# The last value unit of each feed-forward stage, worked through in thirds of the tokens

## The chip, the cores and the metric

The kernel runs on one core of a Trainium2 chip. The metric is the device time of one execution in microseconds (us); lower is better. The time of the kernel before is a median of three runs. Beside them there is one execution that the hardware profiler recorded. The engines are TensorE (PE, matrix products), VectorE (DVE), ScalarE (ACT), GpSimd (POOL) and SyncE (SP, which issues the transfers).

## The reference

One inference step of a decoder of two layers, for 1024 prompt tokens and 8 sample tokens, 1032 columns in all, in float32. Each layer is an attention mixer with a residual, and then a convolutional feed-forward with a residual. The change touches only the feed-forward:

```python
def conv_ffn(hn, conv_state, w_up, conv_w, conv_b, w_down):
    T = hn.shape[1]
    u = hn @ w_up                                             # D 1024 -> 2 * 2816
    uc = jnp.concatenate([conv_state.astype(u.dtype), u], axis=1)
    c = sum((conv_w[j] * uc[:, j:j + T] for j in range(CONV_W)), conv_b)   # causal, width 3
    gate, val = jnp.split(c, 2, axis=-1)
    return (jax.nn.silu(gate) * val) @ w_down, uc[:, T:]
```

## The kernel before

Features lie on the 128 partitions and tokens on the free axis. The residual `hT` is 8 chunks of 128 features by 1032 tokens. A float32 product is made of three matmuls on operands that are split into a high and a low part (`product`, lines 348 to 350: high by high, high by low, low by high), each over one third of the tokens (`TH` = 344 columns, `NT` = 3). The PSUM tensor `acc` has two sets of three banks, `acc_set(0)` and `acc_set(1)`, one bank for each third.

The 2816 inner features are 22 chunks. A feed-forward stage takes them two at a time, in 11 turns; `ffn_pe`, `ffn_act` and `ffn_dve` run the same turn on their engines, ten times as a loop and once, the last (`z.last`), written out. There are two stages, one for each layer. A turn holds four up units (the gate and the value half of two chunks; one unit is 72 matmuls) and two down units. In the last turn three up units are left, numbered 1 (value), 2 (gate) and 3 (value).

What one unit goes through after its matmuls, in the kernel before, always over the full 1032 tokens:

- ACT copies it out of PSUM into `u_ext` (L1090).
- DVE scales it by the norm's `rinv` (L1140), and makes the convolution: one tensor_scalar with the last tap and the bias (L1142), one tensor by scalar plus tensor for each of the two other taps (L1145, L1149), two small ones on the 8 sample tokens (L1147, L1152), and a small copy of the last columns into `u_tail` (L1143).
- For a gate unit ACT then makes the SiLU (L1095) into `ebuf`. For a value unit DVE multiplies it with `ebuf` into `fbuf` (L1159), ACT rounds that into `f_hi` (L1098), and DVE takes the rest into `f_lo` (L1161).

The down products read `f_hi` and `f_lo`. For each of 8 output chunks n and each third t there are three matmuls for the turn's first inner chunk (e = 0) and three for its second (e = 1), into `acc_set(n % 2)`. DVE adds the finished set to `hT` (L882). Chunk n + 2 needs the set that chunk n used, so its matmuls wait for that addition (`h_added`). In the last turn the matmuls of e = 0 for the chunks n = 0 and 1 are issued ahead (`early = 2`), since they need only the first inner chunk; then TensorE waits for `flo_ready` of the second (line 1056) before any matmul of e = 1.

Each engine works strictly in the order of its program; the order is written out by hand, and semaphores carry what waits for what.

Of the kernel before, what the change touches and what calls it, by code (L numbers as in the profile page):

```python
# [29 lines left out]
KC = D // P  # L30
SEQ = 1024
NS = 8
T = SEQ + NS
NT = 3
TH = T // NT
# [77 lines left out]
def build(nc, a, outs):  # L113
    with ExitStack() as ctx:
# [3 lines left out]
        def sem(name):  # L118
            return ctx.enter_context(nc.semaphore(name))
# [52 lines left out]
        tab_in = sem("tab_in")  # L172
        conv_in = sem("conv_in")
        gain_rows_set = sem("gain_rows_set")
        gains_turned = sem("gains_turned")
        gains_set = sem("gains_set")
        tab_turned = sem("tab_turned")
        tab_set = sem("tab_set")
# [29 lines left out]
        up_evac = sem("up_evac")  # L208
        conv_step = sem("conv_step")
        u_scaled = sem("u_scaled")  # L210
        conv_out = sem("conv_out")
        e_ready = sem("e_ready")
        f_raw = sem("f_raw")
# [9 lines left out]
        chain = sem("chain")  # L223

        class Dilated:

# [54 lines left out]
        class Sample:  # L281

            def __init__(self, p, slots):
                self.cols = sem(f"{p}_cols")
                self.cache = [sem(f"{p}_cache{i}") for i in range(slots)]
                self.prep = sem(f"{p}_prep")
                self.moved = sem(f"{p}_moved")
                self.kt = sem(f"{p}_kt")
                self.step = sem(f"{p}_step")
                self.act = sem(f"{p}_act")  # L290
                self.pe = sem(f"{p}_pe")
                self.out = sem(f"{p}_out")
# [4 lines left out]
                self.split = sem(f"{p}_split")  # L297
# [98 lines left out]
        def acc_set(n):  # L396
            return acc[:, 3 * (n % 2):3 * (n % 2) + 3, 0:TH]
# [72 lines left out]
        def rows_in_pe(pe):  # L470
            pe.wait_ge(ident_in, 16)
            for n in range(NTILE + 1):
                pe.wait_ge(x_in[n % XS], 16 * (n // XS + 1))
                if n >= 3:
                    pe.wait_ge(h_set, 2 * (n - 3) + 2)
                rows = P if n < NTILE else NS
                for c in range(KC):
                    mm = pe.transpose(acc[:, (2 * n + c // 4) % 6, P * (c % 4):P * (c % 4) + rows],
                                      x_stage[n % XS][0:rows, P * c:P * c + P], ident[0:rows, 0:rows])
                mm.then_inc(x_turned, 1)  # L480
            pe.wait_ge(tab_in, GAINS_IN)
            pe.transpose(aux[:, 1, 0:46], head_rows, ident[0:46, 0:46])
            pe.transpose(aux[:, 1, 64:64 + 5 * KC], norm_rows, ident[0:5 * KC, 0:5 * KC]) \
                .then_inc(gains_turned, 1)

        def conv_tables_pe(pe, n):

# [20 lines left out]
        def rows_in_dve(v):  # L508

            v.memset(head_rows, 1.0).then_inc(gain_rows_set, 1)  # L510
            for n in range(NTILE + 1):
                v.wait_ge(x_turned, n + 1)
                rows = P if n < NTILE else NS
                for b in range(2):
                    v.tensor_copy(hT[:, 4 * b:4 * b + 4, P * n:P * n + rows],
                                  acc[:, (2 * n + b) % 6, :].rearrange("p (c n) -> p c n", n=P)[:, :, 0:rows]) \
                        .then_inc(h_set, 1)
            v.wait_ge(gains_turned, 1)
# [107 lines left out]
        def third(x, t):  # L626
            return x[:, TH * t:TH * t + TH]
# [386 lines left out]
                body(eng, Turn(l, i, False))  # L1014
            body(eng, Turn(l, LAST, True))

        def up_pe(pe, unit, k):
            slot, u, _ = unit_at(*unit)
            pe.wait_ge(lo_ready, u + 1)
            w1 = w_hi[:, slot, :].rearrange("p (k n) -> p k n", n=P)  # L1020
            w2 = w_lo[:, slot, :].rearrange("p (k n) -> p k n", n=P)
            for t in range(NT):
                for j in range(KC):
                    mm = product(pe, acc_set(k)[:, t, :], w1[:, j, :], w2[:, j, :], third(xh[:, j, :], t),
                                 third(xl[:, j, :], t), j == 0, j == KC - 1)
            mm.then_inc(w_used, 1)

        def ffn_turn_pe(pe, z):
            pe.wait_ge(h_added, z.added - 1)
# [12 lines left out]

            def down(n, e, t):
                s = slots[e]
                return product(pe, acc_set(k0 + n)[:, t, :], w_hi[:, s, P * n:P * n + P],
                               w_lo[:, s, P * n:P * n + P], third(f_hi[:, e, :], t), third(f_lo[:, e, :], t),
                               e == 0, e == 1)


            early = 2 if z.last else 0  # L1050
            pe.wait_ge(flo_ready, z.f + 1)
            for n in range(early):
                pe.wait_ge(up_evac, z.up + n + 3)
                for t in range(NT):
                    down(n, 0, t)
            pe.wait_ge(flo_ready, z.f + 2)
            for n in range(KC):
                if n >= 2:
                    pe.wait_ge(h_added, z.added + n - 1)
                elif not z.last:  # L1060
                    pe.wait_ge(up_evac, z.up + n + 4)
                for t in range(NT):
                    if n >= early:
                        m0 = down(n, 0, t)
                    m1 = down(n, 1, t)
                if n < KC - 1:
                    m1.then_inc(res_full, 1)
                else:
                    m0.then_inc(w_used, 1)
                    m1.then_inc(w_used, 1)  # L1070

        def ffn_pe(pe, l):
            u0 = [U_FFN0, U_FFN1][l]
            pe.wait_ge(lo_ready, u0 + 1)
            *_, mm = normed_product(pe, u0 % RING, 1 + 3 * l)
            mm.then_inc(w_used, 1)
            pe.wait_ge(n_stat, 2 * STAT[1 + 3 * l] + 1)
            turns(pe, l, ffn_turn_pe)

            pe.wait_ge(conv_out, UPS * (l + 1))  # L1080
            pe.wait_ge(tail_set, 2 * l)
# [10 lines left out]
        def gate_act(act, z, e):  # L1092
# [4 lines left out]
            act.wait_ge(w_used, z.no(1))  # L1097
            act.copy(f_hi[:, e, :], fbuf).then_inc(fhi_ready, 1)  # L1098

        def ffn_turn_act(act, z):  # L1100
            split_ahead(act, *z.unit(1))
            up_evac_act(act, z, 1, VAL, 1)
# [4 lines left out]
            up_evac_act(act, z, 3, VAL, 1)  # L1107
            if not z.last:
                split_ahead(act, *z.unit(4))
            gate_act(act, z, 1)  # L1110
            if not z.last:
# [42 lines left out]
        def gated_dve(v, z, e):  # L1154
# [5 lines left out]
            v.wait_ge(fhi_ready, z.f + e + 1)  # L1160
            v.tensor_tensor(f_lo[:, e, :], fbuf, f_hi[:, e, :].bitcast(F32), ALU.subtract).then_inc(flo_ready, 1)  # L1161

        def ffn_turn_dve(v, z):
# [5 lines left out]
            conv_dve(v, l, z.up + 3, VAL, FC + g + 1, s + CONV_STEPS, z.f + 1)  # L1169
            gated_dve(v, z, 1)  # L1170
            s += 2 * CONV_STEPS
            k0 = 0 if z.last else 1
            for n in range(KC):
# [11 lines left out]

        def ffn_dve(v, l):
            for n in range(2):
                v.memset(u_ext[n][:, 0:2], 0.0).then_inc(chain, 1)
            v.wait_ge(chain, 2 * (l + 1))
# [1468 lines left out]
```

## Time and profile before

| | us |
|---|---|
| median of three runs | 2930.18 (2929.76 to 2930.49) |
| profiled execution | 2925.12 |
| its span | 2923.3 |
| TensorE busy in the span | 2695.3 (92%) |
| VectorE busy | 1802.5 (62%) |
| ScalarE busy | 979.7 (34%) |
| GpSimd busy | 729.4 (25%) |

Busy time says how long an engine had an instruction under way. The span is from the first to the last instruction of the profiled execution; 1.8 us of its time lie around it. TensorE's granted clock over the span is 0.951 of its full 2.4 GHz. On this chip it has two levels, 1.2 and 2.4 GHz; at a third of the tokens (344 columns) the matmuls start 0.157 us apart at the upper one and 0.287 us apart at the lower one. The first feed-forward stage's last turn lies around 1640 to 1686 us, the second's around 2855 to 2900 us, just before the rows of the result are turned and written.

### The profile page before, as it was taken

To read this page: it belongs to the slowest core of one execution; us is meant where nothing else is said; L and a number is where in the kernel's file an instruction comes from. 1 tells how busy PE (TensorE), PEld (TensorE's weight loads), DVE (VectorE), ACT (ScalarE), POOL (GpSimd) and SP (SyncE) were. 2 spreads that over 40 slices of the span, in tenths; PEclk is the share of its full clock that TensorE was granted. 3 is DMA by queue.
4 is the path that set the end of the run, shared out by engine and by line. 5 is a ranking of instruction groups with operands and counts; after the bars stand their busy time and mean duration, and the time that the engine had idled before them with its cause. 6 is when DMAs were issued, how large, how long until landed. Compare 5 with 4: busy or idle time off the path is not lost.

```text
span 2923.3 us, 45840 instructions
## 1 busy us (share of the span) xinstructions
PE 2695.3 (92%) x17524; PEld 2626.7 (90%) x17524; DVE 1802.5 (62%) x2804; ACT 979.7 (34%) x1818; POOL 729.4 (25%) x354
## 2 busy tenths in 40 slices
PE   4999999788788999999999969698999999999997
PEld 3999999777778999999999958598999999999996
DVE  6787831555545666666666686795266666666665
ACT  3666632666304211212211245584131111211220
POOL 2111112344302222222222141173222222222220
PEclk7999999888788999999999989898999999999998
DMA  3322233434345333444444111444634444444341
GB/s 105 86 79 85 74 123 95 151 107 113 107 145 113 84 89 84 83 96 95 88 90 92 38 40 59 130 145 127 133 80 89 90 89 85 83 85 93 86 76 61
DMA packets 219857, 275.65 MB, mean 94 GB/s; under 512 B 29562, under 2 KB 191746, under 8 KB 217666
## 3 DMA queue, kind: packets, MB, share of 16 engines
q1 hardware_dynamic: 219746, 274.17, 38.1%
q8 instruction: 70, 1.15, 0.2%
q14 instruction: 41, 0.34, 0.0%
HBM read 237.90 MB, written 125.62 MB: 124 GB/s over the span
## 4 chain that ended last, share of the span: by engine, by line
PE 75%; DVE 9%; issue 5%; ACT 4%; DMA 3%; POOL 2%; SPq 1%; DVEq 0%; ACTq 0%; POOLq 0%
PE acc L348 21%; PE acc L350 21%; PE acc L349 21%; PE aux L2019 2%; DVE arena L609 1%; PE aux L1614 1%; PE acc L2006 1%; DVE f_lo L1161 1%; DVE arena L1140 1%; DVE arena L1159 1%; PE acc L1539 1%; PE acc L1989 1%; PE aux L666 1%; PE aux L665 1%; PE acc L1573 1%
## 5 line engine op out<-in xcount | busy, mean ns | idle before, releaser
L348 PE MATMUL acc<-xh,w_hi 128*128 128x344 f32 x3504 | 1136.8, 324 | 47.4 <-DVE xl L563 21.7
L350 PE MATMUL acc<-xh,w_lo 128*128 128x344 f32 x3504 | 1128.8, 322 | 0.0
L349 PE MATMUL acc<-xl,w_hi 128*128 128x344 f32 x3504 | 1128.5, 322 | 0.0
L333 POOL TENSOR_TENSOR w_lo<-w_raw,w_hi 128x1024 fp32r<-128x1024 f32 x194 | 499.9, 2582 | 1810.4 <-ACT w_hi L323 1810.4
L348 PEld LDWEIGHTS acc<-xh,w_hi 128*128 128x128 f32 x3504 | 666.0, 190 | 61.5 <-issue 31.2
L350 PEld LDWEIGHTS acc<-xh,w_lo 128*128 128x128 f32 x3504 | 666.3, 190 | 0.0
L349 PEld LDWEIGHTS acc<-xl,w_hi 128*128 128x128 f32 x3504 | 665.9, 190 | 0.2
L882 DVE TENSOR_TENSOR hT<-hT,acc 128x1032 f32<-128x1032 f32 x184 | 226.3, 1230 | 388.2 <-PE acc L350 388.2
L323 ACT CAST w_hi<-w_raw 128x1024 fp32r<-128x1024 f32 x194 | 201.8, 1051 | 603.1 <-PE acc L350 515.2
L348 PE MATMUL acc<-f_hi,w_hi 128*128 128x344 f32 x1056 | 342.2, 324 | 29.2 <-DVE f_lo L1161 29.2
L350 PE MATMUL acc<-f_hi,w_lo 128*128 128x344 f32 x1056 | 340.5, 322 | 0.0
L349 PE MATMUL acc<-f_lo,w_hi 128*128 128x344 f32 x1056 | 339.4, 321 | 0.0
L1140 DVE TENSOR_TENSOR arena<-arena,rinv 128x1032 f32<-128x1032 f32 x88 | 146.5, 1665 | 175.9 <-ACT arena L1090 159.7
L1090 ACT COPY arena<-acc 128x1032 f32<-128x1032 f32 x86 | 87.9, 1022 | 446.6 <-PE acc L350 446.6
L1142 DVE TENSOR_SCALAR arena<-arena,cw 128x1032 f32<-128x1032 f32 x88 | 227.5, 2586 | 15.9 <-DVE arena L1140 15.6
L348 PEld LDWEIGHTS acc<-f_hi,w_hi 128*128 128x128 f32 x1056 | 200.3, 190 | 35.4 <-issue 21.2
L350 PEld LDWEIGHTS acc<-f_hi,w_lo 128*128 128x128 f32 x1056 | 200.2, 190 | 0.0
L349 PEld LDWEIGHTS acc<-f_lo,w_hi 128*128 128x128 f32 x1056 | 200.1, 189 | 0.0
L1098 ACT CAST f_hi<-arena 128x1032 fp32r<-128x1032 f32 x44 | 46.5, 1056 | 289.7 <-DVE arena L1159 289.7
L1145 DVE SCALAR_TENSOR_TENSOR arena<-arena,cw 128x1024 f32<-128x1024 f32 x88 | 113.1, 1285 | 4.8
L1149 DVE SCALAR_TENSOR_TENSOR arena<-arena,cw 128x1024 f32<-128x1024 f32 x88 | 113.0, 1284 | 0.2
L1838 ACT ACTIVATE arena<-arena 128x128 f32<-128x128 f32 (+1 forms) x192 | 84.6, 445 | 13.4 <-DVE arena L1679 13.3
(264 smaller groups left out, 3147.3 us busy)
## 6 DMA issues: line engine op xcount, KB each, us to landing
out_a_w_sample<-in_cache_a_kv_w SPq DMA_DIRECT2D x23, 2848.0 KB
w_raw<-in_ffn_w_up SPq DMA_DIRECT2D x88, 512.0 KB, 3.9
scratch<-arena SPq DMA_DIRECT2D x46, 516.0 KB, 3.1
w_raw<-in_ffn_w_down SPq DMA_DIRECT2D x44, 512.0 KB, 3.5
w_raw<-in_a_w_in SPq DMA_DIRECT2D x36, 512.0 KB, 4.3
out_a_w_sample<-in_cache_a_kv_w SPq DMA_DIRECT2D x8, 2044.0 KB
arena<-in_cache_a_kv_w SPq DMA_DIRECT2D x24, 512.0 KB, 3.8
w_raw<-scratch SPq DMA_DIRECT2D x17, 512.0 KB, 3.8
```

What stands on the lines that cost most here:

```text
L323: act.copy(w_hi[:, slot, :], w_raw[:, slot, :]).then_inc(hi_ready, 1)
L333: pool.tensor_tensor(w_lo[:, slot, :], w_raw[:, slot, :], w_hi[:, slot, :].bitcast(F32), ALU.subtract).then_inc(lo_ready, 1)
L348: pe.matmul(out, whi, ahi, start=first, stop=False)
L349: pe.matmul(out, whi, alo, start=False, stop=False)
L350: return pe.matmul(out, wlo, ahi, start=False, stop=last)
L882: v.tensor_tensor(thirds(hT[:, n, :]), thirds(hT[:, n, :]), acc_set(k), ALU.add).then_inc(h_added, 1)
L1090: act.copy(thirds(u_ext[which][:, 2:U1]), acc_set(k)).then_inc(up_evac, 1)
L1140: v.tensor_tensor(u[:, 2:U1], u[:, 2:U1], rinv[:], ALU.mult).then_inc(u_scaled, 1)
L1142: v.tensor_scalar(c[:, 0:T], u[:, 2:U1], w[2], w[3], ALU.mult, ALU.add).then_inc(conv_step, 1)
L1145: v.scalar_tensor_tensor(c[:, 0:SEQ], u[:, 1:SEQ + 1], w[1], c[:, 0:SEQ], ALU.mult, ALU.add) \
L1149: v.scalar_tensor_tensor(c[:, 0:SEQ], u[:, 0:SEQ], w[0], c[:, 0:SEQ], ALU.mult, ALU.add) \
L1838: act.activation(y, y, ACT.Exp, bias=stat_col(i, g, 0, h, t), scale=-1.0, accum_out=stat_col(i, g, 1, h, t)).then_inc(DA.exped, 1)
```

## The change

In the last turn of each stage, the chain behind up unit 3 is done by thirds of the tokens. TensorE signals after each third of the unit (`last_full`). ACT copies third 0 and third 1 out as they are finished, while the unit's later matmuls still run. DVE scales, convolves and multiplies a third, ACT rounds it, DVE subtracts, and TensorE's e = 1 matmuls for n = 0 and 1 are issued by thirds, each with its own wait. The other ten turns, and the chunks n = 2 to 7 of the last one, are as before. The copy into `u_tail` moves to the end of the chain, and the transposes behind the stage wait for it too. Three semaphores that were in use elsewhere are merged or dropped to make room (`gains_turned`, `chain`, an unused one); the steps of the chain count on `ffn_once`.

On VectorE, at the last turn of the second stage, the rows from the scaling of unit 3 to its residual addition read in the kernel before:

```order
L1140 TENSOR_TENSOR arena<-arena,rinv 128x1032 [waits f_raw,up_evac]
L1142 TENSOR_SCALAR arena<-arena,cw 128x1032 [waits u_scaled]
L1143 COPY u_tail<-arena 128x10
L1145 SCALAR_TENSOR_TENSOR arena<-arena,cw 128x1024 [waits conv_step]
L1147 SCALAR_TENSOR_TENSOR arena<-st_T,cw,arena 128x8
L1149 SCALAR_TENSOR_TENSOR arena<-arena,cw 128x1024 [waits conv_step]
L1152 SCALAR_TENSOR_TENSOR arena<-st_T,cw,arena 128x8 [waits conv_step]
L1159 TENSOR_TENSOR arena<-arena 128x1032 [waits flo_ready,e_ready,conv_out]
L1161 TENSOR_TENSOR f_lo<-arena,f_hi 128x1032 [waits fhi_ready]
```

In the changed kernel the five rows of third 0 and the four of third 1's convolution stand ahead (L1226, L1228, L1230, L1233 are the convolution of a third, L1258 its product with the gate), and from the `f_lo` of third 0 (L1266) on it reads:

```order
L1266 TENSOR_TENSOR f_lo<-arena,f_hi 128x344 [waits last_act]
L1258 TENSOR_TENSOR arena<-arena 128x344 [waits flo_ready,e_ready,ffn_once]
L1238 TENSOR_TENSOR arena<-arena,rinv 128x344 [waits up_evac]
L1240 TENSOR_SCALAR arena<-arena,cw 128x344 [waits u_scaled]
L1242 SCALAR_TENSOR_TENSOR arena<-arena,cw 128x336 [waits conv_step]
L1244 SCALAR_TENSOR_TENSOR arena<-st_T,cw,arena 128x8
L1246 SCALAR_TENSOR_TENSOR arena<-arena,cw 128x336 [waits conv_step]
L1248 SCALAR_TENSOR_TENSOR arena<-st_T,cw,arena 128x8 [waits conv_step]
L1266 TENSOR_TENSOR f_lo<-arena,f_hi 128x344 [waits last_act]
L1258 TENSOR_TENSOR arena<-arena 128x344 [waits e_ready,flo_ready,conv_step,conv_out]
L1266 TENSOR_TENSOR f_lo<-arena,f_hi 128x344 [waits fhi_ready]
L1281 COPY u_tail<-arena 128x10
```

Nine rows of the full width have become twenty-one, and the `f_lo` of a third stands one step late, behind the convolution of the next third, so that ACT can round it meanwhile.

On ScalarE, at the same place, the kernel before has the copy out of unit 3, the SiLU of unit 2 and the rounding of unit 3:

```order
L1090 COPY arena<-acc 128x1032 [waits conv_out,w_used]
L1095 ACTIVATE arena<-arena 128x1032 [waits f_raw,conv_out]
L1098 CAST f_hi<-arena 128x1032 [waits w_used,f_raw]
```

and the changed one:

```order
L1130 COPY arena<-acc 128x344 [waits conv_out,last_full] x2
L1146 ACTIVATE arena<-arena 128x1032 [waits f_raw,conv_out]
L1138 CAST f_hi<-arena 128x344 [waits ffn_once,w_used]
L1130 COPY arena<-acc 128x344 [waits conv_out,w_used]
L1138 CAST f_hi<-arena 128x344 [waits ffn_once]
L1138 CAST f_hi<-arena 128x344 [waits f_raw]
```

The SiLU now stands ahead of the copy of the last third, and the rounding of third 0 between them. The core of the diff:

```diff
@@ up_pe: a signal after each third
+                if by_third and t < NT - 1:
+                    mm.then_inc(last_full, 1)
@@ ffn_turn_pe
-            up_pe(pe, z.unit(3), 1)
+            up_pe(pe, z.unit(3), 1, z.last)
...
-            pe.wait_ge(flo_ready, z.f + 2)
-            for n in range(KC):
+            if z.last:
+                for t in range(NT):
+                    if t < NT - 1:
+                        pe.wait_ge(ffn_once, steps(z.l, f"lo{t}"))
+                    else:
+                        pe.wait_ge(flo_ready, z.f + 2)
+                    for n in range(early):
+                        m1 = down(n, 1, t)
+                        if t == NT - 1:
+                            m1.then_inc(res_full, 1)
+            else:
+                pe.wait_ge(flo_ready, z.f + 2)
+            for n in range(early, KC):
                 if n >= 2:
                     pe.wait_ge(h_added, z.added + n - 1)
@@ new on ScalarE
+        def last_half_act(act, z):
+            last_evac_act(act, z, 0)
+            last_evac_act(act, z, 1)
+            act.wait_ge(conv_out, z.up + 3)
+            act.wait_ge(f_raw, z.f + 1)
+            act.activation(ebuf, cg, ACT.Silu).then_inc(e_ready, 1)
+            act.wait_ge(w_used, z.no(1))
+            last_hi_act(act, z, 0)
+            last_evac_act(act, z, 2)
+            last_hi_act(act, z, 1)
+            last_hi_act(act, z, 2)
@@ new on VectorE: the convolution of thirds 0 and 1
+                v.wait_ge(last_act, acts(l, f"evac{t}"))
+                n = steps(l, f"conv{t}")
+                v.tensor_tensor(last_third(u, t), last_third(u, t), third(rinv, t), ALU.mult).then_inc(ffn_once, 1)
+                v.wait_ge(ffn_once, n + 1)
+                v.tensor_scalar(third(c, t), last_third(u, t), w[2], w[3], ALU.mult, ALU.add).then_inc(ffn_once, 1)
+                v.wait_ge(ffn_once, n + 2)
+                v.scalar_tensor_tensor(c[:, a:b], u[:, 1 + a:1 + b], w[1], c[:, a:b], ALU.mult, ALU.add) \
+                    .then_inc(ffn_once, 1)
...
+        def last_half_dve(v, z, ch, s):
+            v.wait_ge(f_raw, z.f + 1)
+            last_conv_dve(v, z, ch, s, 0)
+            last_product_dve(v, z, 0)
+            last_conv_dve(v, z, ch, s, 1)
+            last_lo_dve(v, z, 0)
+            last_product_dve(v, z, 1)
+            last_conv_dve(v, z, ch, s, 2)
+            last_lo_dve(v, z, 1)
+            last_product_dve(v, z, 2)
+            last_lo_dve(v, z, 2)
+            v.tensor_copy(u_tail[:, :, bass.ds(ch, 1)], u_ext[VAL][:, SEQ:U1].unsqueeze(2)).then_inc(ffn_once, 1)
@@ ffn_turn_act and ffn_turn_dve call them where z.last, and the old steps otherwise
```

## Rows read from the trace of the kernel before

**Rows 1.** Waits of TensorE: who waited for whom, us, times, longest.
```profile
PE acc L348 <- DVE f_lo L1161: 29.2, 22, 6.8
```

**Rows 2.** Timeline of TensorE, second stage: start us, us, engine line op [idle before].
```profile
2855.57 0.32 PE L348 MATMUL acc<-xh,w_hi 128*128 128x344 f32 x1
...
2866.75 0.32 PE L350 MATMUL acc<-xh,w_lo 128*128 128x344 f32 x1
...
2869.57 0.32 PE L350 MATMUL acc<-f_hi,w_lo 128*128 128x344 f32 x1
2876.71 0.66 PE L348 MATMUL acc<-f_hi,w_hi 128*128 128x344 f32 x1 [6.82 <-DVE f_lo L1161]
2877.16 0.49 PE L349 MATMUL acc<-f_lo,w_hi 128*128 128x344 f32 x1
```

**Rows 3.** Timeline of VectorE, second stage, same columns.
```profile
2863.45 0.23 DVE L1152 SCALAR_TENSOR_TENSOR arena<-st_T,cw,arena 128x8 f32<-128x8 f32 x1
2868.16 1.23 DVE L1140 TENSOR_TENSOR arena<-arena,rinv 128x1032 f32<-128x1032 f32 x1 [4.49 <-ACT arena L1090]
2869.43 0.82 DVE L1142 TENSOR_SCALAR arena<-arena,cw 128x1032 f32<-128x1032 f32 x1
...
2870.28 1.28 DVE L1145 SCALAR_TENSOR_TENSOR arena<-arena,cw 128x1024 f32<-128x1024 f32 x1
2871.48 0.22 DVE L1147 SCALAR_TENSOR_TENSOR arena<-st_T,cw,arena 128x8 f32<-128x8 f32 x1
...
2873.07 1.23 DVE L1159 TENSOR_TENSOR arena<-arena 128x1032 f32<-128x1032 f32 x1
2875.42 1.23 DVE L1161 TENSOR_TENSOR f_lo<-arena,f_hi 128x1032 fp32r<-128x1032 f32 x1 [1.12 <-ACT f_hi L1098]
2879.70 1.23 DVE L882 TENSOR_TENSOR hT<-hT,acc 128x1032 f32<-128x1032 f32 x1 [3.04 <-PE acc L350]
...
2885.11 1.23 DVE L882 TENSOR_TENSOR hT<-hT,acc 128x1032 f32<-128x1032 f32 x1 [1.61 <-PE acc L350]
```

**Rows 4.** Timeline of ScalarE, second stage, same columns.
```profile
2867.11 1.02 ACT L1090 COPY arena<-acc 128x1032 f32<-128x1032 f32 x1 [9.36 <-PE acc L350]
2868.02 1.07 ACT L1095 ACTIVATE arena<-arena 128x1032 f32<-128x1032 f32 x1
2874.34 1.05 ACT L1098 CAST f_hi<-arena 128x1032 fp32r<-128x1032 f32 x1 [5.24 <-DVE arena L1159]
```

**Rows 5.** Lines with a third's width: duration ns min/median/max, first and last start.
```profile
L698 DVE TENSOR_TENSOR f_lo<-arena,f_hi x99: 516/518/520, 75.6 to 1871.5; 128x344 fp32r<-128x344 f32 x99
L717 DVE TENSOR_TENSOR arena<-aux,rope x99: 503/517/518, 78.9 to 1875.0; 128x344 f32<-128x344 f32 x99
L696 DVE CAST f_hi<-arena x99: 326/332/791, 74.8 to 1871.1; 128x344 fp32r<-128x344 f32 x99
L720 DVE TENSOR_TENSOR arena<-arena x99: 516/518/2564, 79.5 to 1875.6; 128x344 f32<-128x344 f32 x99
L677 ACT ACTIVATE arena<-acc x99: 441/457/460, 73.8 to 1868.0; 128x344 f32<-128x344 f32 x99
L680 ACT CAST f_hi<-arena x99: 478/480/484, 74.8 to 1869.0; 128x344 fp32r<-128x344 f32 x99
```

**Rows 6.** Timeline of GpSimd in the last turns, same columns as rows 2.
```profile
1661.66 2.47 POOL L333 TENSOR_TENSOR w_lo<-w_raw,w_hi 128x1024 fp32r<-128x1024 f32 x1 [16.09 <-ACT w_hi L323]
2857.82 2.50 POOL L333 TENSOR_TENSOR w_lo<-w_raw,w_hi 128x1024 fp32r<-128x1024 f32 x1 [8.83 <-ACT w_hi L323]
```

**Rows 7.** Timeline of VectorE, first stage: the addition of chunk 2.
```profile
1670.26 1.23 DVE L882 TENSOR_TENSOR hT<-hT,acc 128x1032 f32<-128x1032 f32 x1 [1.68 <-PE acc L350]
```

**Rows 8.** Stretches: us, busy (x instructions) by engine, granted clock, DMA share, GB/s.
```profile
908.90:912.70 3.80, 1.82 (x11) 1.40 (x9) 2.91 (x4) 3.80 (x5) 0.00 (x0) 1.00 0.77 96
912.70:914.57 1.87, 0.00 (x0) 0.00 (x0) 1.87 (x3) 1.87 (x3) 0.00 (x0) 1.00 1.54 195
916.10:919.60 3.50, 3.50 (x14) 3.50 (x14) 3.50 (x4) 2.13 (x3) 0.00 (x0) 0.52 1.20 169
1655.10:1660.10 5.00, 0.03 (x1) 0.00 (x0) 4.42 (x7) 0.51 (x1) 0.00 (x0) 1.00 0.00 0
2869.90:2871.90 2.00, 0.00 (x0) 0.00 (x0) 2.00 (x5) 0.00 (x0) 0.00 (x0) 0.99 0.00 0
2871.90:2876.70 4.80, 0.00 (x0) 0.00 (x0) 3.60 (x4) 1.05 (x1) 0.00 (x0) 0.50 0.00 0
2876.70:2882.04 5.34, 5.33 (x19) 5.33 (x20) 1.23 (x1) 0.00 (x0) 0.00 (x0) 0.50 0.00 0
```

More of the change, by code:

```diff
@@ L210, in build, with acts, steps @@
         u_scaled = sem("u_scaled")
+        last_full, last_act, ffn_once = sem("last_full"), sem("last_act"), sem("ffn_once")
+        ACTS = {"evac0": 1, "evac1": 2, "hi0": 3, "hi1": 4}
+        STEPS = {"set": 2, "conv0": 2, "raw0": 7, "conv1": 7, "lo0": 12, "raw1": 13, "lo1": 14, "tail": 15}
+        def acts(l, name):
+            return len(ACTS) * l + ACTS[name]
+        def steps(l, name):
+            return STEPS["tail"] * l + STEPS[name]
         conv_out = sem("conv_out")
@@ L222, in build @@
         copied = sem("copied")
-        chain = sem("chain")
         class Dilated:
@@ L1015, in turns, with up_pe @@
             body(eng, Turn(l, LAST, True))
-        def up_pe(pe, unit, k):
+        def up_pe(pe, unit, k, by_third=False):
             slot, u, _ = unit_at(*unit)
@@ L1080, in ffn_pe @@
             pe.wait_ge(conv_out, UPS * (l + 1))
+            pe.wait_ge(ffn_once, steps(l, "tail"))
             pe.wait_ge(tail_set, 2 * l)
@@ L1098, in gate_act, with last_third, last_evac_act, last_hi_act @@
             act.copy(f_hi[:, e, :], fbuf).then_inc(fhi_ready, 1)
+        def last_third(x, t):
+            return x[:, 2 + TH * t:2 + TH * t + TH]
+        def last_evac_act(act, z, t):
+            if t < NT - 1:
+                act.wait_ge(last_full, (NT - 1) * z.l + t + 1)
+            else:
+                act.wait_ge(w_used, z.no(3) + 1)
+            act.wait_ge(conv_out, z.up + 2)
+            act.copy(last_third(u_ext[VAL], t), acc_set(1)[:, t, :]) \
+                .then_inc(last_act if t < NT - 1 else up_evac, 1)
+        def last_hi_act(act, z, t):
+            if t < NT - 1:
+                act.wait_ge(ffn_once, steps(z.l, f"raw{t}"))
+            else:
+                act.wait_ge(f_raw, z.f + 2)
+            act.copy(third(f_hi[:, 1, :], t), third(fbuf, t)).then_inc(last_act if t < NT - 1 else fhi_ready, 1)
+        def last_half_act(act, z):
[9 more added lines that the diff above has]
+            last_hi_act(act, z, 2)
         def ffn_turn_act(act, z):
@@ L1106, in ffn_turn_act @@
             split_ahead(act, *z.unit(3))
-            up_evac_act(act, z, 3, VAL, 1)
-            if not z.last:
+            if z.last:
+                last_half_act(act, z)
+            else:
+                up_evac_act(act, z, 3, VAL, 1)
                 split_ahead(act, *z.unit(4))
-            gate_act(act, z, 1)
-            if not z.last:
+                gate_act(act, z, 1)
                 up_evac_act(act, z, 4, GATE, 0)
@@ L1161, in gated_dve, with last_conv_dve @@
             v.tensor_tensor(f_lo[:, e, :], fbuf, f_hi[:, e, :].bitcast(F32), ALU.subtract).then_inc(flo_ready, 1)
+        def last_conv_dve(v, z, ch, s, t):
+            l, u, c = z.l, u_ext[VAL], c_out[VAL]
+            w = [cw[:, l, k, bass.ds(ch, 1)] for k in range(4)]
+            state = [st_T[:, l, :, bass.ds(ch + 2 * FC * k, 1)] for k in range(2)]
+            a, b = TH * t, min(TH * t + TH, SEQ)
+            if t < NT - 1:
+                v.wait_ge(last_act, acts(l, f"evac{t}"))
[6 more added lines that the diff above has]
+                    .then_inc(ffn_once, 1)
+                v.wait_ge(ffn_once, n + 3)
+                v.scalar_tensor_tensor(c[:, a:b], u[:, a:b], w[0], c[:, a:b], ALU.mult, ALU.add) \
+                    .then_inc(ffn_once, 1)
+                return
+            cs = c[:, SEQ:T].unsqueeze(2)
+            v.wait_ge(up_evac, z.up + 4)
+            v.tensor_tensor(last_third(u, t), last_third(u, t), third(rinv, t), ALU.mult).then_inc(u_scaled, 1)
+            v.wait_ge(u_scaled, z.up + 4)
+            v.tensor_scalar(third(c, t), last_third(u, t), w[2], w[3], ALU.mult, ALU.add).then_inc(conv_step, 1)
+            v.wait_ge(conv_step, s + 1)
+            v.scalar_tensor_tensor(c[:, a:b], u[:, 1 + a:1 + b], w[1], c[:, a:b], ALU.mult, ALU.add) \
+                .then_inc(conv_step, 1)
+            v.scalar_tensor_tensor(cs, state[1], w[1], cs, ALU.mult, ALU.add).then_inc(conv_step, 1)
+            v.wait_ge(conv_step, s + 2)
+            v.scalar_tensor_tensor(c[:, a:b], u[:, a:b], w[0], c[:, a:b], ALU.mult, ALU.add).then_inc(conv_step, 1)
+            v.wait_ge(conv_step, s + 3)
+            v.scalar_tensor_tensor(cs, state[0], w[0], cs, ALU.mult, ALU.add).then_inc(conv_out, 1)
@@ new lines, in last_product_dve @@
+        def last_product_dve(v, z, t):
+            if t < NT - 1:
+                v.wait_ge(ffn_once, steps(z.l, f"conv{t}") + 4)
+            else:
+                v.wait_ge(conv_out, z.up + 4)
+                v.wait_ge(conv_step, TURN_STEPS * FFN_TURNS * (z.l + 1))
+            v.wait_ge(e_ready, z.f + 2)
+            v.wait_ge(flo_ready, z.f + 1)
+            v.tensor_tensor(third(fbuf, t), third(cv, t), third(ebuf, t), ALU.mult) \
+                .then_inc(ffn_once if t < NT - 1 else f_raw, 1)
@@ L1168, in ffn_turn_dve @@
             conv_dve(v, l, z.up + 2, GATE, g + 1, s, z.f + 1)
-            conv_dve(v, l, z.up + 3, VAL, FC + g + 1, s + CONV_STEPS, z.f + 1)
-            gated_dve(v, z, 1)
+            if z.last:
+                last_half_dve(v, z, FC + g + 1, s + CONV_STEPS)
+            else:
+                conv_dve(v, l, z.up + 3, VAL, FC + g + 1, s + CONV_STEPS, z.f + 1)
+                gated_dve(v, z, 1)
             s += 2 * CONV_STEPS
@@ L1187, in ffn_dve @@
             for n in range(2):
-                v.memset(u_ext[n][:, 0:2], 0.0).then_inc(chain, 1)
-            v.wait_ge(chain, 2 * (l + 1))
+                v.memset(u_ext[n][:, 0:2], 0.0).then_inc(ffn_once, 1)
+            v.wait_ge(ffn_once, steps(l, "set"))
             v.wait_ge(n_stat, 2 * STAT[1 + 3 * l] + 2)
```

13 lines of the change are left out of this document (9 added, 4 removed).

## The prediction, on record before the changed kernel ran

> **What bounds the kernel now.** I read the list of waits of TensorE first, since that engine is busy for 92% of the span and most of the chain that ended last is its matmuls. In it the wait of the first down matmul (L348) for the last step of the feed-forward chain (L1161) is the largest: 29.2 us, 22 times, at most 6.8 us [rows 1]. The 22 are the 11 turns of both stages. The two last turns hold 6.8 us each, 13.6 in all, so the other twenty have 0.8 us each. The change touches only those two.
>
> Then I read the timelines of the second stage's last turn, engine by engine. TensorE starts up unit 3 at 2855.57 and issues the last of its 72 matmuls at 2866.75, 0.157 us apart; 18 matmuls of e = 0 follow, until 2869.57; then nothing until 2876.71 [rows 2]. In that gap everything runs one after another over the full width: copy out on ACT from 2867.11, scaling from 2868.16, three wide steps of the convolution and two small ones, the product from 2873.07, the rounding on ACT from 2874.34, the subtraction from 2875.42 to 2876.65 [rows 3, 4]. Before it VectorE had been idle for 4.49 us, from 2863.68, the end of the gate's convolution [rows 3]: the finished thirds of unit 3 lay in PSUM and nobody took them. That idle time is what the change can use.
>
> The gap costs more than its length. The granted clock falls to 0.50 inside it, and stays there for the first 5.34 us of matmuls, in which 18 are issued 0.287 us apart instead of 0.157 [rows 2, 8]. So 18 x 0.13 = 2.3 us belong to the gap too.
>
> **The change, part by part.** All times are of the second stage.
>
> Durations of a third. A tensor by tensor step takes 0.518 us, a copy from PSUM on ACT 0.457, a rounding on ACT 0.480 [rows 5]. The tensor by scalar plus tensor step takes 1.28 us at 1024 columns and 0.22 at 8 [rows 3]; on the straight line between, 344 columns take 0.57. The trace has no tensor_scalar with two scalars at 344 columns. It is at least 0.33 us, as the cheapest single-input step of that width [rows 5], and at most 0.82, as at 1032 columns with GpSimd idle [rows 3]; I take 0.46: the wide one is 0.41 us below the wide tensor by tensor step, so I give it half of that step's 1.04 ns a column (1.233 less 0.518 over 688 columns), and 688 columns fewer take 0.36 off 0.82. A step that waits for the one before it starts 0.04 us after its end; one that doesn't wait starts 0.08 before it (2869.39 to 2869.43, and 2870.28 + 1.28 against 2871.48) [rows 3].
>
> ACT copies third 0 out near 2859.5 and third 1 at 2863.3 (the unit's thirds are 24 matmuls, 3.77 us, apart, and the last ends at 2867.07) [rows 2]; both are out when VectorE comes free. Then the SiLU, 2863.8 to 2864.9: it used to stand behind the copy and now stands ahead of it, and is ready before third 0 needs it.
>
> VectorE, third 0: scaling from 2863.60, tensor_scalar 2864.16, two taps 2864.66 and 2865.28, product 2865.89 to 2866.41. ACT rounds it until 2866.93 and then copies third 2 out, 2867.11 to 2867.57, as early as before. The rounding stands ahead of that copy: were the product of third 0 later than about 2866.6, the copy would be late; there is 0.2 us of room, then 0.7 until chunk 1's e = 0 matmuls want the bank near 2868.3, and 1.8 until VectorE wants third 2. Third 1: scaling 2866.33, its convolution until 2868.58, the subtraction of third 0 from 2868.50 to 2869.02, the product 2868.94 to 2869.46. Third 2: scaling 2869.38, tensor_scalar 2869.94, the taps with the two small steps until 2871.77, the subtraction of third 1 until 2872.21, the product 2872.13 to 2872.65, rounding until 2873.17, subtraction 2873.21 to 2873.73.
>
> TensorE: third 0 (6 matmuls, 0.94 us) is ready at 2869.02, before e = 0 is through; it goes from 2869.73 to 2870.67. Third 1 from 2872.25 to 2873.2. Third 2 from 2873.78, against 2876.71 before for all 18: the chain is 2.9 us shorter although VectorE does more instructions (21 for 9) and 2.4 us more of work.
>
> The new wait. Chunk 2 needs the set of chunk 0, so it needs its addition. Before, 9 matmuls of chunk 1 covered that: addition 0 began at 2879.70 and chunk 2 at 2882.08 (2885.11 less 0.04, 0.32 and 17 x 0.157) without waiting [rows 3]. Now only 3 matmuls lie between. After a wait the second matmul follows 0.45 us behind instead of 0.287 [rows 2], so I add 0.16. Chunk 0 is full at 2873.78 + 0.16 + 2 x 0.157 + 0.32 = 2874.57, its addition runs 2874.62 to 2875.85 (the tail's copy, 0.17, is over by then), and chunk 2 starts at 2875.90, after about a microsecond of waiting. Queued behind that wait are all other down matmuls, so it counts in full. The addition of chunk 2 then begins at 2875.90 + 0.16 + 17 x 0.157 + 0.36 = 2879.09. It was 2885.11: 6.0 us less, if the clock stays up. From there on both kernels are paced by 18 matmuls a chunk, 2.83 us.
>
> First stage: the same turn 1214.76 us earlier, and its addition of chunk 2 is at 1670.26 [rows 7] against 2879.09 - 1214.76 = 1664.33 now: 5.9 us less. What is different there is the weight split of the next stage's first unit on GpSimd. It runs 2.47 us from 1661.66 [rows 6], behind the last rounding and one cast on ACT, and would run from about 1659.5, over the addition of chunk 0. Steps of VectorE with two SBUF operands are held up by such a thing, up to 2564 ns instead of 518, but the same step with one operand in PSUM never was, 503 to 518 ns over 99 [rows 5]; the addition reads PSUM, so I take 0. In the second stage GpSimd is idle from 2860.32 on [rows 6], ahead of all thirds. The squares of the next norm, the loads and the transposes follow the additions as before and move with them. The transposes' new wait for the tail's copy is met 25 us ahead. The merged semaphores, 20 more signals and the weight loads cost nothing on the path. The copies by thirds on ACT lie in 9.36 us of idle time [rows 4].
>
> Sum: 6.0 + 5.9 = 11.9 us off the profiled execution, 2925.12 to 2913.2. The median of the runs is 5.06 us above that execution; I carry this over: 2930.18 - 11.9 = 2918.2.
>
> **A rule against the rows: the clock.** The pauses that are left are 1.6 us (after third 0), 0.6 (after third 1) and 1.0 (before chunk 2), with 0.94 us of matmuls between. In the trace the clock fell 2.0 us after the last matmul in the second stage and only after 5.0 us in the first [rows 8]. And from 908.9 to 916.1 matmuls with pauses below 2.0 us between them first kept 1.00, then fell to the lower level at about 916.1, behind a pause of 1.87 us [rows 8]. So pauses of this size can cost the clock, but don't have to. The Trainium skill (TensorE: Matmul & The Clock Gate, HAM oscillation) puts the fall behind single idle gaps that are longer than any left here; by it no stage would fall and the time is the 2918.2 of the sum. The row at 916.1 does not agree with that, and by it one stage in three may fall. I go by the row for the chances, and by no fall in either stage for the likeliest.
>
> **The rivals.** (1) The clock falls in one stage or both, between third 0 and chunk 2. Price: 5.34 us were needed to get it back [rows 8], in which 18 matmuls lose 0.13 each: 2.4 us a stage. 2920.6 for one, 2923.0 for both. For it: the row at 916.1. Against: more matmuls stand in the gap than there.
> (2) The small steps cost more than their widths say (waits that cross engines at each third, the tensor_scalar at 0.82). 21 steps at 0.1 us more make third 2 2.1 us late, 4.2 us over both stages: 2922.4. For it: nothing here shows these shapes with three semaphores on one step. Against: the hand-overs of 0.04 us.
> (3) The gain of the first stage is lost behind it, in the transfers and stores between the layers: only 6.0 us remain, 2924.2. Against: that part starts by semaphores from the last addition, and no transfer is waited for within it before the projections.
> (4) Slower than before. The clock falls in the first pause and does not come back while chunks 2 to 7 run, because each of them now starts on a TensorE that has just waited. Price: 0.13 us for each of their 108 matmuls, 14.0 us a stage, against the 6.0 gained; from 46 matmuls at the low clock on the stage loses. One stage: 2930.18 - 11.9 + 14.0 = 2932.3. Against it: in both stages of before the clock came back within 5.4 us of unbroken matmuls, and from chunk 3 on nothing breaks them.
> (5) That the thirds change nothing, since VectorE was not free: excluded by its 4.49 us of idle time.
>
> **How the numbers follow.** Forecast with no fall in either stage 0.43; (1) 0.36, of which 0.28 for one stage; (2) 0.10; (3) 0.07; (4) 0.04. Below about 0.2% (5.9 us) a measurement of this kernel can't tell a change from none. Faster by more: the forecast, (1) and (2), 0.89. Within: (3) and a mixture of (1) and (2), 0.07. Slower: 0.04. The range: if the tensor_scalar takes its 0.33 and the 0.16 after a wait is hidden, a stage gains 0.6 more, 2917.0, and 1 us for the scatter of the median gives 2916.0. Above it takes in both falls and half of (2): 2923.6.
>
> **What would show it.** In the profile after, the wait of TensorE for L1161's place should fall from 6.8 us a stage to two waits of about 1.6 and 0.6, and a new one of 1.0 for the addition of chunk 0 appears. The step of third 0 should be over before e = 0 is through, third 2 should be ready 2.9 us earlier, and 12 of the 18 matmuls should lie ahead of it. The granted clock should stay at 1.00 from 2855 to the rows' output. The addition of chunk 2 should come 6.0 us earlier. It is wrong if a wide wait stays (VectorE's steps dearer), if the clock drops, or if the two stages gain unequally.

## The result, and the profile after

| | before | changed |
|---|---|---|
| median, us | 2929.97 (8 runs, 2927.93 to 2932.99) | 2918.37 (8 runs, 2913.69 to 2925.10) |
| ratio | | 0.9959, 95% interval 0.9950 to 0.9968 |
| profiled execution | 2925.12 | 2924.54 |

The changed kernel is 11.6 us faster, by the medians; the interval allows 9.4 to 14.6. The change was compared twice more: 2917.91 against 2933.40 (ratio 0.9963, interval 0.9935 to 0.9992) and 2918.73 against 2929.51 (0.9956, 0.9940 to 0.9972), 15.5 and 10.8 us by the medians.

The two profiled executions differ by 0.6 us only, and a reader who compared their spans would find no gain. Single executions of one kernel scatter by several us, in parts of the program that the change doesn't touch. The start of the copy of unit 2 in the first stage's last turn is a mark for that. It lies ahead of everything that is done by thirds; of the change only the merged semaphores lie earlier. It is at 1641.02 us in the first trace of before, 1645.15 in a second one, 1647.78, 1649.09 and 1643.03 in three of the changed kernel; over all 14 traces of this study it lies between 1640.8 and 1652.7. One stretch in which the traces part, in the trace of before, in a second trace of before and in that of the changed kernel (stretch, busy by engine, then granted clock, DMA share, GB/s):

```profile
840.00:930.00 90.00, 81.85 (x500) 80.03 (x501) 30.35 (x37) 26.23 (x27) 12.06 (x6) 0.86 0.52 128
```
```profile
840.00:930.00 90.00, 79.25 (x478) 76.51 (x479) 32.06 (x44) 22.73 (x25) 11.95 (x5) 0.82 0.50 128
```
```profile
840.00:930.00 90.00, 77.67 (x471) 75.03 (x472) 33.53 (x48) 22.23 (x24) 12.63 (x6) 0.81 0.50 130
```

In all 14 traces the mark is later, the fewer matmuls lie in this stretch: from 502 and 1640.8 us down to 454 and 1652.7. From 930 to 1640 us all of them have the same work at a clock of 1.00. So this scatter arises ahead of 930 us, 700 us before the changed turn, and kernels with and without the change are mixed along the row.

So I measure the change where it acts: in each stage's last turn, from the start of the copy of up unit 2 to the start of the addition of chunk 2. I call this the stretch. In the second stage of before it is 2855.77 to 2885.11, 29.34 us, and 29.24 in the first. VectorE in the second stage of the changed kernel (start us, us, engine, line; ahead of these, third 0 began at 2869.37 right behind the gate's convolution):

```profile
2874.21 0.52 DVE L1266 TENSOR_TENSOR f_lo<-arena,f_hi 128x344 fp32r<-128x344 f32 x1
2874.64 0.51 DVE L1258 TENSOR_TENSOR arena<-arena 128x344 f32<-128x344 f32 x1
2875.07 0.51 DVE L1238 TENSOR_TENSOR arena<-arena,rinv 128x344 f32<-128x344 f32 x1
2875.61 0.46 DVE L1240 TENSOR_SCALAR arena<-arena,cw 128x344 f32<-128x344 f32 x1
2876.11 0.57 DVE L1242 SCALAR_TENSOR_TENSOR arena<-arena,cw 128x336 f32<-128x336 f32 x1
...
2878.83 0.52 DVE L1266 TENSOR_TENSOR f_lo<-arena,f_hi 128x344 fp32r<-128x344 f32 x1 [0.55 <-ACT f_hi L1138]
2879.26 0.17 DVE L1281 COPY u_tail<-arena 128x10 f32<-128x10 f32 x1
2880.17 2.37 DVE L888 TENSOR_TENSOR hT<-hT,acc 128x1032 f32<-128x1032 f32 x2 [0.74 <-PE acc L356]
2884.59 1.23 DVE L888 TENSOR_TENSOR hT<-hT,acc 128x1032 f32<-128x1032 f32 x1 [2.05 <-PE acc L356]
```

These answer to [rows 3]. VectorE has no idle time of 4.49 us any more. The last subtraction ends at 2879.35, and the copy of unit 2 began at 2861.55 in this trace, 5.78 us later than in that of before. With this taken off ("on the clock of before", below), the end is 2873.57, against 2876.65: 3.1 us earlier. The stretch is 23.04 us. TensorE around it:

```profile
2876.32 0.32 PE L356 MATMUL acc<-f_hi,w_lo 128*128 128x344 f32 x1
2877.91 0.43 PE L354 MATMUL acc<-f_hi,w_hi 128*128 128x344 f32 x1 [1.28 <-DVE f_lo L1266]
...
2879.40 0.42 PE L354 MATMUL acc<-f_hi,w_hi 128*128 128x344 f32 x1 [0.29 <-DVE f_lo L1266]
2879.66 0.32 PE L355 MATMUL acc<-f_lo,w_hi 128*128 128x344 f32 x1
...
2881.45 0.42 PE L354 MATMUL acc<-f_hi,w_hi 128*128 128x344 f32 x1 [0.85 <-DVE hT L888]
```

One pause of 6.82 us [rows 2] has become three, before third 1, before third 2, and before chunk 2, which waits for the addition of chunk 0. (The times in brackets count from the end of the last matmul, which a profile models, and so come out 0.16 us below a pause counted from when the next matmul could have started.) In the first stage the same three stand (1.27, 0.28 and 0.46), but the clock falls in the middle, 0.4 us after the matmuls of third 2 have begun. Stretches of the first stage, then of the second (us, busy PE, PEld, DVE, ACT, POOL, granted clock, DMA, GB/s):

```profile
1662.70:1666.00 3.30, 1.75 (x10) 1.30 (x9) 2.41 (x8) 1.43 (x2) 0.00 (x0) 1.00 0.00 0
1666.00:1669.40 3.40, 2.94 (x11) 2.50 (x10) 2.37 (x2) 1.50 (x2) 2.38 (x1) 0.51 0.00 0
2876.50:2882.00 5.50, 3.08 (x16) 2.39 (x16) 4.22 (x10) 0.48 (x1) 0.00 (x0) 1.00 0.00 0
```

The first stage's stretch is 24.00 us, from 1647.78 to 1671.78. The two stages gain 5.24 and 6.30, together 11.54 us.

Does this reach the end of the program? From the start of the copy of unit 2 in the second stage to the end of the span it is 67.4 to 67.7 us in three traces whose second stage is as before, and 61.2 to 61.3 in four whose second stage works by thirds: 6.2 us less, all of it. From that copy in the first stage to the one in the second it is 1214.7 to 1217.3 us in three traces with the first stage as before, and 1210.7 to 1213.8 in four with the first stage by thirds. The means are 3.9 us apart, with a scatter of 3 us in each group, so this shows that the first stage's gain gets through, but not how much of it.

### The profile page after: what moved, and what is told of

Read it like the earlier page. It is cut to its first block, busy times and chain, and to the rows that moved or that the text cites. A ratio compares the mean times of both kernels' runs of the same rounds, so it can differ in the third digit from the quotient of the medians.

```text
span 2922.8 us, 45882 instructions
## 1 busy us (share of the span) xinstructions
PE 2701.8 (92%) x17524; PEld 2633.1 (90%) x17524; DVE 1804.8 (62%) x2828; ACT 982.1 (34%) x1826; POOL 729.3 (25%) x354
## 4 chain that ended last, share of the span: by engine, by line
PE 74%; DVE 10%; issue 5%; ACT 3%; DMA 3%; POOL 2%; SPq 1%; DVEq 0%; ACTq 0%; POOLq 0%
PE acc L354 21%; PE acc L356 21%; PE acc L355 20%; PE aux L2142 2%; PE aux L1737 1%; DVE arena L615 1%; PE acc L1662 1%; PE acc L2129 1%; DVE arena L1194 1%; PE acc L1705 1%; PE acc L2112 1%; PE aux L672 1%; DVE f_lo L1215 1%; DVE arena L1213 1%; PE aux L671 1%
```

## The experiments

The stretches below are read from each kernel's own trace, as above. Before, in two traces: 29.24 and 28.94 in the first stage, 29.34 and 29.41 in the second. The second trace was taken in the expectation that the stretch repeats within 0.2 us; in the first stage it moved by 0.3.

**The changed kernel again.** No edit.

> The changed kernel once more, for its scatter and a second trace. My theory (each stage gains about 6: third 2 is ready 2.9 us earlier, 12 of 18 matmuls lie ahead of it, the low clock behind the stall goes, one new wait of about 1 us): 11 to 12 us below the kernel before. If the scatter of the single executions (2914 to 2925) comes from this change, the two stages' last turns will differ by several us from those of the first trace; if it comes from elsewhere, they repeat within 1.2 us (the price of one short stay at the low clock) and the differences lie in the attention parts.

> The changed kernel beside the three variants below, on one chip: stretch 24.0 and 23.1 us again, and a third look at whether the clock falls in the first stage's pauses and not in the second's.

Medians as above. Stretches 23.99 and 23.08, then 23.11 and 23.06. So the change's own part repeats within 0.1 us but for the first stage, where the clock fell in two traces of three and not in the third: 24.0 or 23.1. The third trace was expected to show the fall again and did not. The mark ahead of the change moved by 6 us meanwhile. The scatter of the executions is from elsewhere.

**One stage only.** The condition `z.last` of the new code is made `z.last and z.l == 0`, or `== 1`; the counts of the semaphores follow.

> Thirds in the first stage's last turn only, the second stage as before. My theory: 5.2 to 5.9 us below the kernel before (2924.5). Rival, that what the first stage gains is lost again in the transfers and waits between the layers: 0 to 1 us below.

> Thirds in the second stage's last turn only. My theory: 6.0 us below the kernel before (2924.2). Rival, that the first stage gives nothing and all of the gain is here: 11 us below.

Measured 2925.16 and 2927.63 against 2933.40: ratios 0.9971 (0.9951 to 0.9991) and 0.9976 (0.9958 to 0.9994), 8.2 and 5.8 us. Stretches 23.99 and 29.23 in the one, 29.26 and 23.04 in the other: each stage gains where it is changed and only there. The intervals of the times are wide, but the first stage's gain does reach the end: the rival that it is lost between the layers would have wanted a ratio of 0.9997 or more there. The other rival, 11 us from the second stage alone, lies inside the second interval (1.8 to 12.3 us) and is refuted by the stretches, not by the time.

**TensorE waits for the whole second chunk.**

```diff
+            pe.wait_ge(flo_ready, z.f + 2)
             if z.last:
-                for t in range(NT):
... (the waits and the issue by thirds)
-            for n in range(early, KC):
+                pe.wait_ge(ffn_once, steps(z.l, "lo1"))
+            for n in range(KC):
```

The matmuls of e = 1 are then issued chunk by chunk, as before.

> ACT and VectorE work by thirds as in the change, but TensorE takes the second inner chunk only when all its thirds are there, and then chunk by chunk as before. The pause of TensorE is then one of 3.9 us instead of 6.8, with all 18 matmuls behind it, and no wait for the first addition. My theory: the shorter chain alone gives 2.9 us a stage; if the low clock goes as well, 5.3 us a stage. So 5.8 us below the kernel before if the clock still falls in both, 10.6 if in neither. Rival, that the issue by thirds is the larger part of the gain: no more than 5.8 below even where the trace shows the clock at 1.00.

Measured 2925.90 against 2933.40, ratio 0.9976 (0.9953 to 0.9999), 7.5 us. Stretches 25.41 and 25.35: 3.9 us a stage, between my two values. The trace of the second stage says why:

```profile
2876.50:2880.40 3.90, 0.18 (x3) 0.01 (x1) 3.28 (x10) 0.63 (x2) 0.00 (x0) 1.00 0.00 0
2880.40:2882.00 1.60, 1.60 (x9) 1.60 (x10) 0.03 (x1) 0.00 (x0) 0.00 (x0) 0.94 0.00 0
2882.00:2885.40 3.40, 3.40 (x14) 3.40 (x14) 1.80 (x2) 0.00 (x0) 0.00 (x0) 0.53 0.00 0
```

The clock falls, but not in the pause: 1.4 us after the matmuls have begun again (0.4 in the first stage), so that 12 matmuls run at the lower level and not 18: 1.6 us and not 2.3. Both theories missed that the price depends on where the fall lies. The last subtraction ends at 2873.56 on the clock of before, as in the change. 29.34 less 3.1 for the chain less 0.8 for the six matmuls more at the upper level is 25.4, as measured. So the shorter chain alone is half of the gain. The rival, a small gain even with the clock at 1.00, was not put to the test, since the clock fell in both stages. The stretch of the change with the clock up, 23.06, is 2.3 us below this: 1.6 for the clock, and 0.7 left for the 12 matmuls that lie ahead (1.9) less the new wait and the restarts.

**The clock by itself.** In the kernel before, after the e = 0 matmuls of the last turn:

```diff
+            def filler(count):
+                for _ in range(count):
+                    pe.matmul(aux[:, 0, 0:TH], w_hi[:, slots[0], 0:P], third(f_hi[:, 0, :], 0), start=True, stop=True)
...
+            if z.last:
+                filler(42)
             pe.wait_ge(flo_ready, z.f + 2)
```

> The kernel before, with 42 matmuls of no use (6.6 us, into a free PSUM bank) in the pause of each last turn, nothing else. They shorten no chain. My theory: the clock stays at 1.00 and the 18 matmuls behind are issued 0.157 us apart; the stretch becomes 26.9 us in both stages, 4.6 us in all below before. So 2.3 of the 6 us a stage are the clock's. Rival, that the low clock only accompanies the stall and costs nothing of its own (VectorE sets the pace behind it): 29.2 still.

Measured 2923.80 against 2932.48, ratio 0.9973 (0.9955 to 0.9991), 8.7 us, with 4.6 inside the interval (2.6 to 13.2). Stretches 27.16 and 27.10. The chain is as long as ever, and TensorE meets its end with the clock up:

```profile
2883.82 1.74 PE L1052 MATMUL aux<-f_hi,w_hi 128*128 128x344 f32 x10
2885.77 0.42 PE L348 MATMUL acc<-f_hi,w_hi 128*128 128x344 f32 x1 [0.21 <-DVE f_lo L1167]
2886.03 0.32 PE L349 MATMUL acc<-f_lo,w_hi 128*128 128x344 f32 x1
2886.19 0.32 PE L350 MATMUL acc<-f_hi,w_lo 128*128 128x344 f32 x1
```

So 2.1 to 2.2 us of each stage's stretch of 29.3 were the clock's (1.8 to 2.3 by the second trace of before), and the rival that it costs nothing is refuted. Behind the stage this trace does not keep all of it: from the copy of unit 2 to the end of the span it is 66.7 us against 67.5, because one transfer was issued 1.7 us behind the one before it, where the same one follows after 0.4 us in before. That is one issue in one trace, and no run says what held it up.

**The splitting without the overlap.**

```diff
 def last_evac_act(act, z, t):
     if t < NT - 1:
         act.wait_ge(last_full, (NT - 1) * z.l + t + 1)
-    else:
-        act.wait_ge(w_used, z.no(3) + 1)
+    act.wait_ge(w_used, z.no(3) + 1)
```

> As the changed kernel, but ACT copies all three thirds out only after the whole of unit 3 (the wait of third 2 also ahead of thirds 0 and 1). So the splitting stays and the overlap with unit 3 goes. My theory: the chain of 10.1 us now starts at 2867.56 instead of 2863.60 and ends 1.1 us later than before's; 12 matmuls lie ahead of its end, so the stretch is 27.1 us with the clock up and up to 29.5 with it down. 0 to 4.4 us below before in all. Rival, that splitting into thirds alone gives the gain: a stretch of 25 us or less.

Measured 2926.17 against 2932.48, ratio 0.9979 (0.9962 to 0.9996), 6.3 us. Stretches 27.25 and 27.16. TensorE's waits in the second stage (us, times, longest):

```profile
PE acc L354 <- ACT arena L1129: 3.0, 1, 3.0
PE acc L354 <- DVE f_lo L1265: 1.1, 2, 0.8
PE acc L354 <- DVE hT L888: 0.9, 1, 0.9
```

and the end of its chain on VectorE:

```profile
2868.41 0.52 DVE L1225 TENSOR_TENSOR arena<-arena,rinv 128x344 f32<-128x344 f32 x1 [4.03 <-ACT arena L1129]
...
2877.87 0.52 DVE L1265 TENSOR_TENSOR f_lo<-arena,f_hi 128x344 fp32r<-128x344 f32 x1 [0.55 <-ACT f_hi L1137]
```

The idle time of VectorE is back. The copy of unit 2 is at 2856.48 here, so the chain ends at 2877.68 on the clock of before, 1.0 us later than the whole-width one, as worked out, and 4.1 us later than in the change. Some 2.1 us of the gain stay without overlap; the other 4.1 a stage (27.16 less 23.06) come from taking the thirds while the unit still runs. The rival, a stretch of 25 us or less, is refuted. What I had not seen is the wait of 3.0 us: chunk 1's e = 0 matmuls need the bank set, and the copy of third 2 now stands behind the rounding of third 0, which waits for VectorE. The clock fell as well, in the first stage by the end of this wait, in the second 0.8 us behind it:

```profile
2872.90:2875.90 3.00, 3.00 (x12) 2.79 (x11) 2.93 (x8) 0.48 (x1) 0.00 (x0) 0.52 0.01 3
```

Yet the stretches are those of my sum with the clock up (27.1). Behind the slow matmuls TensorE still waited 0.8 us (0.6 in the first stage) for the subtraction of third 1, so their slowness went into that wait. Here a low clock cost nothing, since nothing waited for these matmuls.

**What the new wait and the fall of the clock cost.** Three variants of the changed kernel. In the first the addition of chunk 0 is done in two parts, third 0 in VectorE's idle 0.55 us ahead of the last subtraction; in the second 8, 2 and 5 matmuls of no use stand in the three pauses; the third has both (8, 2 and 3).

```diff
... (a signal behind chunk 0's third 0 on PE; ACT counts 3 signals a stage, not 2)
             last_product_dve(v, z, 2)
+            v.wait_ge(last_full, NT * z.l + NT)
+            h = third(hT[:, 0, :], 0)
+            v.tensor_tensor(h, h, acc_set(0)[:, 0, :], ALU.add)
             last_lo_dve(v, z, 2)
... (the later addition of chunk 0 takes its thirds 1 and 2 only)
@@ PE, behind the e = 1 matmuls of each third
+                    filler((8, 2, 3)[t])
```

> Only the addition of chunk 0's third 0 is put ahead, no matmuls of no use. My theory: 0.35 us less in each stage: stretch 23.7 and 22.7, with the clock low for some 3.4 us in the first stage as in the change. Rival, that the shorter pause alone keeps the clock up: 22.7 in both.

> Only the matmuls of no use (8, 2 and 5) are put into the pauses of the changed kernel. My theory: the clock stays at 1.00 in both stages and the stretch is 23.1 in both: 0.9 us less in the first stage, none in the second. Rival, that the fall in the first stage has another cause than the pauses: 24.0 still.

> The changed kernel with two additions. VectorE adds third 0 of chunk 0 to the residual in the 0.55 us in which it waits for the last rounding, so that the addition that chunk 2 waits for covers 688 columns instead of 1032 (0.88 us instead of 1.23); and 8, 2 and 3 matmuls of no use are put into TensorE's three pauses (their results are not read). My theory: the stretch is 22.7 us in both stages, 1.6 us less than the change in all. Rival, that the matmuls of no use delay the next wait's end or that the clock falls all the same: 24 us in the first stage.

> Both together, once more, against the changed kernel on the same chip. The stretches were 22.78 and 22.69 us. My theory: 1.6 us below the changed kernel, which the times of whole executions (scatter of 3 to 5 us) can hardly tell; the stretches can.

| | stretch 1 | stretch 2 | median | ratio to before |
|---|---|---|---|---|
| changed kernel | 23.11 | 23.06 | 2918.73 | 0.9956 (0.9940 to 0.9972) |
| addition ahead | 22.78 | 22.69 | 2916.00 | 0.9948 (0.9931 to 0.9965) |
| filled | 23.14 | 23.07 | 2914.67 | 0.9941 (0.9926 to 0.9956) |
| both | 22.79 | 22.69 | 2917.72 | 0.9952 (0.9937 to 0.9968) |
| both, on another chip | 22.78 | 22.69 | 2918.43 | 0.9948 (0.9932 to 0.9964) |

The first four rows are from one chip and share one measurement of before. The addition ahead is worth 0.33 to 0.37 us a stage, as expected; TensorE's new wait is down to 0.5 us:

```profile
2868.66 0.50 DVE L1284 TENSOR_TENSOR hT<-hT,acc 128x344 f32<-128x344 f32 x1
2869.28 0.52 DVE L1268 TENSOR_TENSOR f_lo<-arena,f_hi 128x344 fp32r<-128x344 f32 x1
2869.72 0.17 DVE L1286 COPY u_tail<-arena 128x10 f32<-128x10 f32 x1
2870.64 0.87 DVE L1308 TENSOR_TENSOR hT<-hT,acc 128x688 f32<-128x688 f32 x1 [0.75 <-PE acc L356]
2871.56 0.43 PE L354 MATMUL acc<-f_hi,w_hi 128*128 128x344 f32 x1 [0.49 <-DVE hT L1308]
```

In its trace the clock stayed up in both stages, so it doesn't say what the short pause does to the clock: the changed kernel's own third trace stayed up too. The expectation that it would be low there was wrong. The useless matmuls delay nothing (23.07 against 23.06). In none of the six last turns of the three filled traces did the clock fall; in the ten changed turns without filling (three traces of the change, the kernel with the addition ahead, and one turn in each kernel with one stage) it fell in three, all of them first stages (three of five; none of the five second stages). That is what the filling should do, but six turns don't prove it, and why only first stages fell stays open. By the whole executions none of the variants can be told from another: their intervals overlap.

## Why the prediction was right

- Predicted 2918.2 in a range of 2916.0 to 2923.6, measured 2918.37. The sum was 6.0 and 5.9 us; the stretches gave 6.30 and 5.24. The mechanism held. That the median lies within 0.2 us of the forecast is luck: its interval spans 5 us (2915.3 to 2920.6), and even the time forecast for one fall of the clock, 2920.6, lies at its edge.
- By its own signs of being wrong the prediction failed in one: the clock drops. The granted clock was to stay at 1.00, and in the first stage it did not, in two traces of three. The two stages gain unequally for that reason.
- The chain. The end of the last subtraction was put at 2873.73, on the clock of before, and came at 2873.57. The six matmuls of third 0 ran before it was needed, right behind those of e = 0, and 12 of the 18 lay ahead of the last third. The durations of a third, taken from other lines of the same width, held: 0.51 or 0.52 us for two tensors, 0.57 or 0.58 for the taps, 0.448 for the copy, 0.483 for the rounding. The unseen tensor_scalar, bounded by 0.33 and 0.82, took 0.458; 0.46 was chosen.
- The idle time of VectorE as the source of the gain: shown by the kernel with late copies, which keeps the splitting and loses 4.1 of 6.3 us while its chain ends 4.1 us later.
- The clock's 2.3 us a stage: shown by the filled kernel before, 2.1 to 2.2. (The prediction has the same 18 matmuls at 2.3 in one place and at 2.4 in another; the product is 2.3.)
- The new wait for the addition of chunk 0: about a microsecond was expected, 0.85 us was read. The restart behind a wait was priced at 0.16 us, from rows at the lower clock, and took 0.10 at the upper (2879.40 to 2879.66, less 0.157).
- GpSimd's split over the first stage's addition, taken at 0: it ran from 1666.05 to 1668.43, and the two additions from 1666.57 took 2.37 us together, as without it.
- Rival 1, the clock. It did fall, in the first stage of two traces in three, and in three of the ten such turns counted above. The row at 916.1, a single place, had suggested one in three; ten turns don't confirm a frequency. (The pause ahead of that row was 2.01 us from the end of the last matmul; the 1.87 is the length of the window that was put into it.)
- The Trainium skill (TensorE: Matmul & The Clock Gate, HAM oscillation) puts the fall behind a single long idle gap, and by it no stage would have fallen. The three first stages that fell do not agree with it: the longest pause ahead was 1.27 us.
- The price of that fall was mis-sized: 0.9 us (24.00 against 23.11), not 2.4. The clock was low for 3.4 us and not 5.3, TensorE stood waiting for the addition in a part of that, and 9 matmuls started in it. The four of chunk 0 and chunk 1 that came first made chunk 2 start only 0.17 us later, and the five of chunk 2 the other 0.7. So the forecast's own case and rival 1 lie 0.9 us apart and not 2.4.
- Rivals 2 and 3, dearer small steps and a gain lost behind the first stage: refuted by the durations and by the kernel with the first stage only. Rival 4, the clock low until the end: in no trace.
- The upper end of the range does not follow from its words. Both falls (4.8 us) and half of rival 2 (2.1) above 2918.2 are 2925.1, not 2923.6. The measured time lies far below either.
- The sum was set against one profiled execution, and the profile after has nearly the same span. The time came out because the same 5.06 us were put back on. "The addition of chunk 2 should come 6.0 us earlier" is true only when counted from a mark within the turn.

What stays open: what moves the executions by up to 12 us ahead of the first changed turn. It happens ahead of 930 us, and fewer matmuls between 840 and 930 us go with it; the granted clock there alone does not order the traces (0.84 in the latest, 0.81 in earlier ones). No run tests it. Open too is what makes the clock fall behind pauses as short as 1.3 us in one execution and not in the same turn of another.

## What to carry to other kernels

In this kernel it paid, and it can be tried elsewhere: when a chain of full-width steps runs behind a unit of matmuls while the engine of its longest part is idle beforehand, cut the last unit along the free axis and start on the first part; the fixed cost of more instructions (here 2.4 us more of VectorE work) is small against idle time that is used (4.49 us). A stall of TensorE can be worth more than its length, since the clock's low stretch may come on top: here 6.8 us of pause cost another 2.2. Count for that only the slow matmuls that something waits for. And when executions scatter by more than the gain, compare the traces from a mark inside the changed stretch: here it repeated within 0.1 us where the clock stayed up, and within 0.3 where it fell in the long pause.

## What the hardware showed that was not expected

The clock was low for 3.4 us in the kernel whose TensorE waits for the whole chunk and in the first stage of the changed one, though the longest pauses ahead were 3.7 us and 1.3 us; behind the pause of 6.8 us it stayed low for 5.34 us of matmuls [rows 8]. In the former the fall came 0.4 and 1.4 us after the matmuls had begun again, not in the pause, and in the second stage of the kernel with late copies 0.8 us after. So a low clock can be met in a stretch that is itself busy. And where TensorE has to wait anyway behind that stretch, as with the late copies, 10 to 12 slow matmuls cost nothing that could be measured.
